# A decoder trunk on one core: the input projection multiplies x scaled by channel weights alone, and one triangular update moves ahead of a scan

## The chip, the cores and the metric

The kernel runs on one core of a Trainium2 chip. Its engines work side by side and meet at semaphores: TensorE (PE) multiplies into eight PSUM banks, VectorE (DVE), ScalarE (ACT) and GpSimd (POOL) work elementwise, SyncE (SP) issues the DMAs. The metric is the device time of one execution, in microseconds.

## What is computed

One decoder layer in float32 on 256 tokens of 1024 channels. This case is about its first part, the mixing block:

```
h = rms_norm(x, norm_pre_mix)        # x * rsqrt(mean(x*x) + 1e-6) * gain
proj = h @ w_in
u_s5, p_ml, p_rw, p_mb = split_cols(proj, (GW, ML_COLS, RW_COLS, MB_COLS))
y = concat(s5_mixer(u_s5), mlstm_mixer(p_ml), rwkv7_mixer(p_rw), moba_mixer(p_mb))
x = x + rms_norm(rms_norm_per_group(y) @ w_out, norm_post_mix)
```

Every mixer begins with work that is linear in its part of `proj`: RWKV mixes each token with the one before it, the mLSTM has a short convolution, S5 a recurrence whose states come from a scan. Attention to 256 memory tokens and a gated feed-forward block follow.

## The kernel before

**Split products.** Each large float32 product is made of three cheaper ones. An operand is split into a rounded `high` (a ScalarE copy) and a `rest` = value - high (a VectorE subtraction), and `mm3` multiplies high by high, high by rest and rest by high. Weights come in slots of 1 MB, loaded by SyncE into a ring of two slots up to `S_WOUT`. A slot is two halves; `high_part` (L344, ScalarE) and `rest` (L350, VectorE) split a half, and `split_channel_major` multiplies it in 24 matmuls of 256 columns. A slot of the ring is loaded again when both of its halves have a rest. Small products (RWKV's solve, S5, the gates) are plain float32.

**The order** is written by hand, engine by engine, and each engine works strictly in it. `highs(n)` and `rests(n)` put the splits of weight halves below n at a place of it. Halves 0 to 17 belong to `rw_wag`, `rw_k`, `rw_r`, `rw_v`, `s5_u`, `ml_q`, `ml_k`, `ml_v`, `ml_o`; from `H_MID` = 18 come `mb_q`, `mb_k`, `mb_v` and the memory's projections.

**The start.** SyncE loads x, two small tables, the first two slots, the rest of the tables. ScalarE and VectorE square x and add its tiles (L362), one TensorE product sums over channels, ScalarE makes the inverse root `rstd_x`, VectorE multiplies x by gain and root in place (L1487), x is split (L1106, L1483), and TensorE begins `rw_wag`.

**Projected groups.** TensorE fills a bank; `shifted` (ScalarE, L1059) copies it times 1 - mu; `mix` (VectorE, L1513) adds the token before; then the bank is free. `conv_now` and `conv_back` do likewise for `ml_q` and `ml_k`.

**RWKV's triangular solve** doubles block sizes over six levels. `level_p` (TensorE) multiplies masked blocks (masks by GpSimd, `level_mask`), `level_x` multiplies them into X and its transpose T, and `level_update` (VectorE, L1656 and L1658) subtracts these from `X` and `XT`. `level_p(2, 0)` needs `level_update(1)`'s first two subtractions: bank 5 holds X of chunk 0 and bank 4 its transpose. `level_x(1, ...)` makes them just before.

**S5.** For each of four pairs: a product, `rotate` (GpSimd), `scan` (VectorE, L1627 and L1628), `rotate_back` (GpSimd, L1006), `s5_out` (TensorE).

## Time and profile before

| what | us |
|---|---|
| median of 3 runs | 527.93 |
| lowest and highest | 526.81, 528.66 |
| the profiled execution | 526.82 |
| its span in the profile | 525.0 |

TensorE is busy for 489.0 us of the span (93%), VectorE for 378.7, ScalarE for 261.2, GpSimd for 172.1. The profile names engines PE, DVE, ACT, POOL and SP; L with a number is a line of the kernel. Matmuls overlap, so their pace is the distance between starts, not a duration.

### The profile page before, as it was taken

Reading aid. Unit: us, or ns where it says so; the run is one execution under the profiler, and the core shown is the slowest. Engines: PE = TensorE matmul, PEld = TensorE weight load, DVE = VectorE, ACT = ScalarE, POOL = GpSimd, SP = SyncE. Lnnn points to the kernel's source line nnn. Section 1 sums busy time; section 2 is a strip of 40 time slices with the busy share of each in tenths; the row PEclk is TensorE's granted clock in tenths of the full one; section 3 lists DMA queues with packets and bytes.
Section 4 is the critical chain, followed back from the end, with each engine's and each line's share of the span. In section 5 each row is a group of like instructions: output and inputs, shape, how many; then the busy total and the mean of one; then the engine's idle time right before and its main releaser. Section 6 shows DMA issues by size and latency. Waiting matters only on the chain.

```text
span 525.0 us, 8449 instructions
## 1 busy us (share of the span) xinstructions
PE 489.0 (93%) x3478; PEld 447.8 (85%) x3478; DVE 378.7 (72%) x443; ACT 261.2 (50%) x410; POOL 172.1 (33%) x103
## 2 busy tenths in 40 slices
PE   0799999889999999999999995999999999999986
PEld 0789989788898888878999884999999999988874
DVE  5675897997766987679655457589999999962114
ACT  3598774331633244657945547454444443443333
POOL 0030317397669250000000001254433443353440
PEclk9999999989999999999999997899999999999999
DMA  8837328022041023535545241356445555545602
GB/s 345 365 96 248 120 93 308 1 81 81 9 153 53 31 81 116 205 99 223 191 171 201 80 150 40 132 199 236 168 161 168 196 198 180 205 161 196 222 0 81
DMA packets 12358, 79.33 MB, mean 151 GB/s; under 512 B 1440, under 2 KB 2080, under 8 KB 3488
## 3 DMA queue, kind: packets, MB, share of 16 engines
q1 hardware_dynamic: 12320, 78.79, 42.3%
q8 instruction: 28, 0.46, 0.4%
q14 instruction: 10, 0.08, 0.1%
HBM read 76.95 MB, written 1.84 MB: 150 GB/s over the span
## 4 chain that ended last, share of the span: by engine, by line
PE 83%; DVE 9%; ACT 3%; issue 2%; DMA 1%; POOLq 0%; POOL 0%; SPq 0%; DVEq 0%; ACTq 0%
PE bank L369 81%; DMA ring<-weights 1%; DVE arena L1635 1%; DVE vx L1662 1%; ACT w_high L344 1%; DVE arena L1452 1%; PE bank L857 1%; POOLq L89 0%; POOL w_rest L350 0%; DVE arena L1627 0%; DVE we_rest L350 0%; DVE arena L1628 0%; DVE wk_rest L350 0%; DVE arena L1806 0%; DVE wm_rest L350 0%
## 5 line engine op out<-in xcount | busy, mean ns | idle before, releaser
L344 ACT ACTIVATE w_high<-ring 128x1024 fp32r<-128x1024 f32 x70 | 73.6, 1058 | 79.7 <-PE bank L369 79.7
L369 PE MATMUL bank<-h_high,w_high 128*128 128x256 f32 x384 | 103.0, 284 | 0.0
L369 PE MATMUL bank<-h_rest,w_high 128*128 128x256 f32 x352 | 99.7, 283 | 0.0
L369 PE MATMUL bank<-h_high,w_rest 128*128 128x256 f32 x320 | 90.7, 283 | 0.0
L350 DVE TENSOR_TENSOR w_rest<-ring,w_high 128x1024 fp32r<-128x1024 f32 x42 | 53.5, 1279 | 44.2 <-ACT w_high L344 44.1
L350 POOL TENSOR_TENSOR w_rest<-third_slot,w_high 128x1024 fp32r<-128x1024 f32 x11 | 26.5, 2407 | 161.4 <-ACT w_high L344 161.4
L350 POOL TENSOR_TENSOR w_rest<-ring,w_high 128x1024 fp32r<-128x1024 f32 x22 | 53.6, 2438 | 74.8 <-ACT w_high L344 74.8
L369 PEld LDWEIGHTS bank<-h_high,w_high 128*128 128x128 f32 x384 | 71.7, 192 | 0.5 <-issue 0.4
L369 PEld LDWEIGHTS bank<-h_rest,w_high 128*128 128x128 f32 x352 | 67.6, 192 | 0.0
L369 PE MATMUL bank<-arena 128*128 128x128 f32 (+7 forms) x496 | 59.4, 300 | 6.5 <-DVE arena L1658 4.5
L369 PEld LDWEIGHTS bank<-arena 128*128 128x128 f32 (+3 forms) x496 | 52.9, 183 | 12.6 <-DVE arena L1658 5.1
L369 PEld LDWEIGHTS bank<-h_high,w_rest 128*128 128x128 f32 x320 | 61.5, 192 | 0.0
L344 ACT ACTIVATE w_high<-third_slot 128x1024 fp32r<-128x1024 f32 x30 | 31.2, 1055 | 28.6 <-PE bank L369 28.6
L369 PE MATMUL bank<-h_high,we_high 128*128 128x256 f32 x128 | 38.3, 299 | 5.7 <-DVE h_rest L1483 5.7
L1452 DVE RECIPROCAL fft<-fft 128x512 f32<-128x512 f32 (+1 forms) x12 | 37.0, 3087 | 0.4
L369 PE MATMUL bank<-h_rest,we_high 128*128 128x256 f32 x128 | 37.3, 291 | 0.0
L369 PE MATMUL bank<-h_high,we_rest 128*128 128x256 f32 x128 | 37.2, 291 | 0.0
L350 DVE TENSOR_TENSOR w_rest<-third_slot,w_high 128x1024 fp32r<-128x1024 f32 x19 | 23.8, 1262 | 17.0 <-ACT w_high L344 17.0
L369 PE MATMUL bank<-w_high,act_high 128*128 128x512 f32 x88 | 34.5, 392 | 1.5 <-POOL w_rest L350 1.5
L369 PE MATMUL bank<-w_rest,act_high 128*128 128x512 f32 x88 | 34.3, 390 | 0.0
L369 PE MATMUL bank<-w_high,act_rest 128*128 128x512 f32 x88 | 34.3, 389 | 0.0
L369 PEld LDWEIGHTS bank<-h_high,we_high 128*128 128x128 f32 x128 | 25.7, 201 | 7.2 <-issue 7.1
(308 smaller groups left out, 1227.2 us busy)
## 6 DMA issues: line engine op xcount, KB each, us to landing
ring<-weights SPq DMA_DIRECT2D x50, 1024.0 KB, 4.9
third_slot<-weights SPq DMA_DIRECT2D x15, 1024.0 KB, 4.9
cst<-consts SPq DMA_DIRECT2D x1, 1664.0 KB, 12.3
gain<-gains SPq DMA_DIRECT2D x3, 512.0 KB, 5.9
par<-params SPq DMA_DIRECT2D x1, 1168.0 KB, 14.6
kx<-x_t SPq DMA_DIRECT2D x1, 1024.0 KB, 4.9
vx<-mem_t SPq DMA_DIRECT2D x1, 1024.0 KB, 10.3
xres<-x_rows SPq DMA_DIRECT2D x1, 1024.0 KB, 10.5
```

The costliest lines, as they stand in the source:

```text
L344: nc.scalar.activation(split_half(i)[0], raw_half(i), ACT.Copy).then_inc(S["w_high"], 1)
L350: e.tensor_tensor(rest_, raw_half(i), high.bitcast(F32), ALU.subtract).then_inc(rest_done(i)[0], 1)
L369: return nc.tensor.matmul(out_, lhsT, rhs, start=start, stop=stop, skip_group_check=True)
L857: last = nc.tensor.transpose(o[:, k, :], xtmp[:, m, c * P:(c + 1) * P], const("ident"))
L1452: return v.reciprocal(x, x)
L1635: v.tensor_tensor(v3(A[:, i, :], 256), v3(o[:, :], 256), copies(mask2, 2), ALU.mult).then_inc(free_of(f"A{i}"), 1)
L1662: last = v.scalar_tensor_tensor(mem_h[:, k, :], mem_h[:, k, :], prm("norm_mem")[:, k:k + 1], rstd_m, ALU.mult, ALU.mult)
```

## The change

**The input norm.** rms_norm of a token is a factor of that token alone, so `proj` = root x ((x x gain) @ w_in). The change splits x x gain directly, in eight tiles of 256 columns (`x_high`, `x_rest`), and gives the root to the projected groups. `x_scale` (VectorE, in place in PSUM) multiplies `rw_wag`, `rw_k`, `rw_r`, `rw_v`, `ml_q`, `ml_k`, `gates` and `ml_o`, and ScalarE's shift, convolution or exponential of the group waits for it. `project_scaled` (VectorE) takes the place of ScalarE's copies of `s5_u` and `mb_k`. The groups whose rows are tokens (`ml_v`, `mb_v`) and the scores of `mb_q` get the root as a column, `rstd_col` and `q_col`, made from two more products of one column. `w_gate` is multiplied by the gain once.

**The start.** The parameters and `onehot` (33 rows) come first, then x and slot 0 in halves, slot 1, the table with `ones`, slot 2, the other constants, slot 3, the other parameters; memory comes with slot 6. TensorE's four `rel` products stand first. The sum over x's squares comes between the halves of `rw_k`, in bank 2. The memory's square moves behind ScalarE's sines, its sum behind `ml_q`.

**Moves in the solve.** `level_update(1)` stands ahead of `rests(H_MID + 4)` and `scan(0)`; GpSimd's `level_mask(3)` ahead of `rotate_back(0)`; `solution(1)` ahead of S5's sigmoid; the product `gn_s5` one step of `w_out` later.

Order of TensorE, start of the program, before (`we0` to `we3` are buffers of w_in halves; numbered banks):

```order
L369 MATMUL bank0<-arena,cst 128x256 [waits x_summed,first_in]
L369 MATMUL bank1<-h_high,we0_high 128x256 [waits h_rest,w_rest_even]
...
L369 MATMUL bank1<-h_high,we1_high 128x256 [waits h_rest,w_rest_odd]
...
L369 MATMUL bank0<-h_high,we2_high 128x256 [waits w_rest_even,bank_free0]
...
L369 MATMUL bank0<-h_high,we3_high 128x256 [waits w_rest_odd]
...
L369 MATMUL bank4<-cst,par 128x384 [waits params_in,consts_in]
```

and in the change:

```order
L378 MATMUL bank4<-cst,par 128x384 [waits onehot_in,first_in]
...
L378 MATMUL bank1<-h_high,we0_high 128x256 [waits h_rest,w_rest_even]
...
L378 MATMUL bank1<-h_high,we1_high 128x256 [waits h_rest,w_rest_odd]
...
L378 MATMUL bank0<-h_high,we2_high 128x256 [waits w_rest_even]
...
L378 MATMUL bank2<-arena,cst 128x256 [waits x_summed,ones_in]
L378 MATMUL bank2<-cst,arena 128x1 x2
L378 MATMUL bank0<-h_high,we3_high 128x256 [waits w_rest_odd]
```

The sum over squares no longer stands ahead of the projection; the `rel` products do.

Order of VectorE between `ml_k` and RWKV's products, before:

```order
L350 TENSOR_TENSOR we0_rest<-ring,we0_high 128x1024 [waits w_high]
L1610 TENSOR_TENSOR arena<-arena 128x512 [waits rw_E,rw_k2]
...
L350 TENSOR_TENSOR wk_rest<-ring,wk_high 128x1024 [waits w_high]
L1618 SCALAR_TENSOR_TENSOR arena<-arena,par 128x256 [waits rw_tilde]
...
L1635 TENSOR_TENSOR arena<-bank4,cst 128x512 [waits bank_full4]
```

and in the change (L1529 is `x_scale`, on `ml_k`, `gates` and `ml_o`):

```order
L1529 TENSOR_TENSOR bank1<-bank1,arena 128x512 [waits bank_full1,rstd_x]
L359 TENSOR_TENSOR we0_rest<-ring,we0_high 128x1024 [waits w_high]
L1582 SCALAR_TENSOR_TENSOR arena<-bank1,par,arena 128x255 [waits bank_full1,ml_cur]
...
L1529 TENSOR_TENSOR bank2<-bank2,arena 36x256 [waits bank_full2,rstd_x]
...
L1687 SCALAR_TENSOR_TENSOR arena<-arena,par 128x256 [waits rw_tilde]
...
L1529 TENSOR_TENSOR bank1<-bank1,arena 128x512 [waits bank_full1,rstd_x]
L1705 TENSOR_TENSOR arena<-bank4,cst 128x512 [waits bank_full4]
```

Three scalings have come in, and the first stands between `ml_k` and the weight half that follows it.

Order of VectorE at the first level update (L1627 and L1628 are the scan's), before:

```order
L1662 SCALAR_TENSOR_TENSOR vx<-vx,par,arena 128x256 [waits rstd_m]
...
L1627 SCALAR_TENSOR_TENSOR arena<-small,arena 128x256 [waits rotating]
L1628 SCALAR_TENSOR_TENSOR arena<-small,arena 128x256
...
L350 TENSOR_TENSOR wm_rest<-ring,wm_high 128x1024 [waits w_high]
L350 TENSOR_TENSOR wk_rest<-ring,wk_high 128x1024 [waits w_high]
L1656 TENSOR_TENSOR arena<-arena,bank5 128x512 [waits bank_full5]
```

and in the change:

```order
L1732 SCALAR_TENSOR_TENSOR vx<-vx,par,arena 128x256 [waits rstd_m]
...
L359 TENSOR_TENSOR wm_rest<-ring,wm_high 128x1024 [waits w_high]
L1726 TENSOR_TENSOR arena<-arena,bank5 128x512 [waits bank_full5]
L1728 TENSOR_TENSOR arena<-arena,bank4 128x512 [waits bank_full4]
...
L359 TENSOR_TENSOR wk_rest<-ring,wk_high 128x1024 [waits w_high]
L1697 SCALAR_TENSOR_TENSOR arena<-small,arena 128x256 [waits rotating]
```

Four scans and a weight split now stand behind the update.

The diff, cut to its core:

```diff
+            def x_high(k):
+                a.activation(h_split[0][:, k, :], hT[:, k, :], ACT.Copy,
+                             scale=prm("pre_mix")[:, k:k + 1]).then_inc(S["h_high"], 1)
+            for k in range(4):
+                x_high(k)
+            highs(1)
+            act.wait_ge(S["x_high_in"], 16)
+            for k in range(4, KD):
+                x_high(k)
+            highs(2)
+            x_square(0)
+            highs(4)
+            x_square(1)
+            a.activation(step, prm("log_step"), ACT.Exp).then_inc(S["s5_step"], 1)
+            highs(5)
...
+            def x_scale(name, rows_=P, n=2):
+                dve.wait_ge(S["rstd_x"], 1)
+                o = v3(wait_full(dve, name)[0:rows_, 0:n * T], T)
+                v.tensor_tensor(o, o, copies(rstd_x[0:rows_], n), ALU.mult).then_inc(S["x_scaled"], 1)
+            def project_scaled(name, out_):
+                o = v3(wait_full(dve, name)[:, :], T)
+                v.tensor_tensor(out_, o, copies(rstd_x, 2), ALU.mult).then_inc(free_of(name), 1)
...
+            x_scale("ml_q")
             rests(14)
...
             rests(16)
+            x_scale("ml_k")
+            rests(17)
             conv_back(1, "ml_k")
-            rests(17)
+            x_scale("gates", GATES, 1)
...
+            rests(H_MID + 3)
+            level_update(1)
+            rests(H_MID + 4)
             scan(0)
-            rests(H_MID + 4)
-            level_update(1)
...
             rests(H_WKV + 10)
+            solution(1)
+            rests(H_WKV + 11)
             dve.wait_ge(S["s5_exp"], 1)
```

## Rows read from the trace of the kernel before

**Rows 1.** TensorE's waits, whole span: waiter <- releaser: us in total, times, longest

```profile
PE bank L369 <- DVE arena L362: 9.6, 1, 9.6
PE bank L369 <- DVE h_rest L1483: 5.7, 1, 5.7
PE bank L369 <- DVE arena L1658: 4.5, 2, 4.0
...
PE bank L857 <- DVE xtmp L1880: 2.4, 1, 2.4
...
PE bank L369 <- DVE arena L1752: 1.3, 1, 1.3
...
PE bank L369 <- ACT arena L1229: 0.8, 1, 0.8
```

**Rows 2.** the chain that ended last, whole span: start us, us, what

```profile
8.89 1.06 ACT we_high L344
...
16.42 35.73 PE bank L369 x257
```

**Rows 3.** DMA issues, 0 to 60 us: count, KB each, us to landing

```profile
kx<-x_t SPq DMA_DIRECT2D x1, 1024.0 KB, 4.9
...
par<-params SPq DMA_DIRECT2D x1, 56.0 KB, 4.4
```

**Rows 4.** timeline (start us, us, engine, line), `rw_wag`'s matmuls at each rate

```profile
17.20 0.42 PE L369 MATMUL bank<-h_high,we_high 128*128 128x256 f32 x1
...
17.41 0.41 PE L369 MATMUL bank<-h_rest,we_high 128*128 128x256 f32 x1
...
22.00 0.28 PE L369 MATMUL bank<-h_high,we_high 128*128 128x256 f32 x1
...
22.11 0.28 PE L369 MATMUL bank<-h_rest,we_high 128*128 128x256 f32 x1
```

**Rows 5.** TensorE's timeline of 30 to 33.5 us, the `rel` products

```profile
30.36 2.84 PE L369 MATMUL bank<-cst,par 33*128 33x384 f32 x8
```

**Rows 6.** ScalarE's timeline, 20 to 60 us; in brackets the idle before, its releaser

```profile
24.91 0.82 ACT L1059 ACTIVATE arena<-bank,small 128x256 f32<-128x256 f32 x2
25.62 2.00 ACT L344 ACTIVATE we_high<-ring 128x1024 fp32r<-128x1024 f32 x2
...
52.17 1.57 ACT L1146 ACTIVATE arena<-bank,small 128x256 f32<-128x256 f32 x4 [2.18 <-PE bank L369]
```

**Rows 7.** VectorE's timeline, around 57 us

```profile
57.44 2.36 DVE L350 TENSOR_TENSOR we_rest<-ring,we_high 128x1024 fp32r<-128x1024 f32 x2 [0.83 <-ACT we_high L344]
```

**Rows 8.** VectorE's timeline, 60 to 100 us

```profile
84.39 4.87 DVE L1635 TENSOR_TENSOR arena<-bank,cst 128x512 f32<-128x512 f32 x8 [2.53 <-PE bank L369]
```

**Rows 9.** VectorE's timeline, 100 to 107 us

```profile
99.96 0.68 DVE L1627 TENSOR_TENSOR_SCAN arena<-small,arena 128x256 f32<-128x256 f32 x1
...
102.31 1.19 DVE L350 TENSOR_TENSOR wm_rest<-ring,wm_high 128x1024 fp32r<-128x1024 f32 x1
103.42 2.28 DVE L350 TENSOR_TENSOR wk_rest<-ring,wk_high 128x1024 fp32r<-128x1024 f32 x1
...
106.22 0.67 DVE L1658 TENSOR_TENSOR arena<-arena,bank 128x512 f32<-128x512 f32 x1
```

**Rows 10.** TensorE's timeline, fp32 level products ahead of the wait and behind it

```profile
99.14 3.84 PE L369 MATMUL bank<-arena 128*128 128x128 f32 x32
...
106.95 3.64 PE L369 MATMUL bank<-arena 128*128 128x128 f32 x16 [3.97 <-DVE arena L1658]
```

**Rows 11.** stretches: PE, PEld, DVE, ACT, POOL busy, granted clock, DMA share, GB/s

```profile
107.00:108.00 1.00, 1.00 (x5) 1.00 (x6) 1.00 (x2) 0.00 (x0) 1.00 (x1) 0.50 0.35 123
204.00:206.00 2.00, 0.73 (x12) 0.66 (x13) 2.00 (x5) 1.54 (x2) 0.00 (x0) 1.00 0.00 0
322.00:323.00 1.00, 0.81 (x4) 0.85 (x5) 1.00 (x3) 1.00 (x2) 0.00 (x0) 0.50 0.00 0
```

**Rows 12.** GpSimd's timeline, 60 to 210 us: turning S5's first pair back

```profile
102.46 7.10 POOL L1006 TENSOR_TENSOR arena<-arena 128x512 f32<-128x512 f32 x4 [2.71 <-DVE arena L1628]
```

More of the change, by code:

```diff
@@ L302, in wait_slot, with scaled @@
             return slot(n)
+        SCALED = ["rw_wag", "rw_k", "rw_r", "rw_v", "ml_q", "ml_k", "gates", "ml_o"]
+        def scaled(eng, name):
+            eng.wait_ge(S["x_scaled"], SCALED.index(name) + 1)
+            return bank[uses[name][0]]
         half_user = {}
@@ L575, in _ @@
                 mm(o[:, 0:384], prm("rel", 33)[:, h:h + 1].to_broadcast([33, P]), const("onehot", 33)).then_inc(full[4 + h], 1)
-            split_channel_major(2, "rw_r", 1, h_split)
-            o = pe_open(pe, "mem_sumsq", 7)
-            pe.wait_ge(S["mem_summed"], 3)
-            mm(o[:, 0:T], const("ones"), sq_m[:, 0, :]).then_inc(full[7], 1)
+            split_channel_major(0, "rw_wag", 1, h_split, lambda j: pe.wait_ge(S["h_rest"], j + 1))
+            split_channel_major(1, "rw_k", 0, h_split, None, (0,))
+            o = pe_open(pe, "x_sumsq", 2)
+            pe.wait_ge(S["ones_in"], 16)
+            pe.wait_ge(S["x_summed"], 3)
+            mm(o[:, 0:T], const("ones"), sq_x[:, 0, :])
+            for m in range(2):
+                last = mm(o[:, T + m:T + m + 1], sq_x[:, 0, m * P:(m + 1) * P], const("ones")[:, 0:1])
+            last.then_inc(full[2], 1)
+            split_channel_major(1, "rw_k", 0, h_split, None, (1,))
+            split_channel_major(2, "rw_r", 3, h_split)
             split_channel_major(3, "rw_v", 0, h_split)
@@ L597, in _ @@
             split_channel_major(5, "ml_q", 0, h_split)
+            o = pe_open(pe, "mem_sumsq", 7)
+            pe.wait_ge(S["mem_summed"], 3)
+            mm(o[:, 0:T], const("ones"), sq_m[:, 0, :]).then_inc(full[7], 1)
             o = pe_open(pe, "rw_kk", 3)
@@ L1165, in _ @@
             a.activation(rwE[:, 2], Gp, ACT.Exp, scale=-1.0).then_inc(S["rw_E"], 1)
-            o = wait_full(act, "gates")
+            o = scaled(act, "gates")
             a.activation(rows[0][0:NH, :], o[32:32 + NH, 0:T], ACT.Identity,
@@ L1186, in _ @@
             a.activation(E_[:, 0:1024], flat(cv), ACT.Tanh, scale=0.5).then_inc(S["ml_silu"], 1)
-            o = wait_full(act, "ml_o")
+            o = scaled(act, "ml_o")
             a.activation(mlo, v3(o[:, :], T), ACT.Exp, scale=-1.0).then_inc(free_of("ml_o"), 1)
@@ L1201, in _ @@
             highs(H_MID + 5)
-            project("mb_k", mqk[:, 2:4, :])
             highs(H_MID + 6)
@@ L1529, in conv_back @@
                     last.then_inc(S["ml_conv"] if d < 3 else free_of(name), 1)
+            rests(5)
+            x_scale("rw_wag")
             mix(0, "rw_wag")
             rests(6)
+            x_scale("rw_k")
             mix(1, "rw_k")
@@ L1541, in _ @@
             v.tensor_scalar(rwE[:, 0, 1, :], rwE[:, 0, 1, :], 0.5, 0.5, ALU.mult, ALU.add).then_inc(S["rw_lowrank"], 1)
+            x_scale("rw_v")
+            rests(11)
             mix(3, "rw_v")
             rests(12)
+            dve.wait_ge(S["consts_in"], 16)
+            dve.wait_ge(S["params_in"], 16)
+            w_gate = v3(prm("w_gate"), GATES)
+            v.tensor_tensor(w_gate, w_gate, spread(prm("pre_mix"), GATES), ALU.mult).then_inc(S["gate_gain"], 1)
             moved(dve, "rw_k")
@@ L1620, in _ @@
             last.then_inc(S["rw_bonus"], 1)
+            x_scale("ml_o")
             def scan(q):
@@ L1691, in _ @@
             rests(H_MID + 6)
+            project_scaled("mb_k", mqk[:, 2:4, :])
             scan(1)
@@ L1817, in _ @@
             v.tensor_tensor(z5, z5y, z5b, ALU.mult).then_inc(S["s5_z"], 1)
-            rests(H_WKV + 11)
-            solution(1)
             group_gain(1, "ml")
```

147 lines of the change are left out of this document (81 added, 66 removed).

## The prediction

> **What bounds the kernel now.** I began with TensorE's waits [rows 1]. TensorE is the busiest engine, and the time that it lacks sits in few places: 9.6 and 5.7 us at the start, 4.0 us (the longest of two) at the level update, and short waits after. Then I read the chain [rows 2]: nothing but TensorE stands in it from 16.42 us on for 35.73 us, so the start is bound by what makes the first operands, and the next 35 us by TensorE's own pace. The last view is the timeline of the engines that feed it. ScalarE works almost without a pause from 24.91 to 50.0 us (52.17 less its 2.18 of idle, [rows 6]), and VectorE from 57.44 us to 81.86 (84.39 less 2.53, [rows 7, 8]). So both feeders have little room, and that decides what an earlier start is worth.
>
> **The start.** The parameters (56 KB, 4.4 us to landing though behind x, [rows 3]) now go first, so the `rel` products begin at 4.0 to 5.1 us. At the higher rate they took 2.8 us [rows 5]. The first matmuls here come 0.21 us apart, later ones 0.11 to 0.12 [rows 4]: 256 columns at 1.2 GHz, then near 2.4. So `rel` takes some 5.6 us and ends at about 10. Half of x, issued 0.9 us later than all of it before (landed 0.72 + 4.9, [rows 3]), is there by 5.5. Four `x_high` at 0.41 us (half of 0.82, [rows 6]), one weight half at about 1.0 (half of 2.00, [rows 6]) and its rest at 1.2 (half of 2.36, [rows 7]) end at 9.2. `rw_wag` begins at 10 instead of 16.42, probably at the full clock, since `rel` has worked for 5.6 us by then, about as long as it took before. Added to `rel` out of the way later (2.8) and 2.2 us of slow matmuls, the lead of TensorE's stream would be 11 us, if the feeders kept up.
>
> They don't. The root now comes late: ScalarE does eight tiles, four halves and two squares first (14.3 us), VectorE its three sums by 17.4, TensorE reaches the product at 18.6, and the root is there at 20.5. `x_scale` on a 512-column bank is costed at 0.61 us, from VectorE's nearest row that reads PSUM (4.87 for 8, [rows 8]); writing PSUM is in no row, so 0.4 to 1.0. ScalarE's shift of `rw_wag` then starts at 21.2, against 24.91 before [rows 6]: 3.7 us of lead. One weight half is already split: +1.0. At `rw_v` ScalarE waits for VectorE, which has `rests(9)`, a mix and `rests(10)` ahead of that scaling: -1.1. The memory's square is moved in here: -1.9. The tanh of `rw_w` so comes at 50.0 - 3.6 + 1.9 = 48.3 us (52.17 before), and `ml_q` starts 4.0 us earlier than before, not 11.
>
> TensorE gets gaps in between: about 3 us ahead of `rw_v`, 2 ahead of `s5_u`, 3 ahead of `rw_g`. The trace shows what gaps do to the clock: after idles of 3.97 us [rows 10] and 2.4 us [rows 1] the granted clock is 0.50, the 1.2 GHz level; after 1.3 us it stayed 1.00 [rows 1, 11]. The gap ahead of `rw_g` is nearest to these longer ones, and `ml_q` behind it is waited for. The loss there is taken as 1.5 us, what the level products show below. The Trainium skill says so too ("TensorE: Matmul & The Clock Gate", HAM oscillation): an array left idle is throttled to half rate and has to be worked warm again. By that rule the gaps cost time, and the trace agrees at 3.97 us.
>
> So `ml_q` is full at 55.7 + 1.5 = 57.2, its scaling ends at 57.8, and `rests(14)` behind it starts 0.4 us later than its 57.44 [rows 7]. From there VectorE has its 24.4 us of work as before, plus the scalings of `ml_k`, `gates` and `ml_o` (0.6, 0.25, 0.6), plus 1.7 us: ScalarE can shift `ml_k` only behind the scaling, and the weight half that `rests(17)` needs comes after that shift. It reaches the first RWKV bank at 85.4 us against 84.39 [rows 8]: **+1.0**. The whole lead of the start is gone there. What hid such a delay before, 2.53 us of idle [rows 8], is used up.
>
> **The level update.** Before, VectorE ran the scans (99.96 to 102.31: 2.35 us), two rests (1.1 and 2.2) and only then the four subtractions, the second of which (106.22 + 0.67) released TensorE at 106.95 [rows 9, 10]. Now the scans and the second rest stand behind. The second subtraction ends at 106.9 + 1.0 - 2.35 - 2.2 = 103.3. TensorE itself gets there at 99.14 + 3.84 = 102.98 [rows 10], plus 1.0. So it goes on at 104.0, bound by its own stream: **-2.9**. And its clock: 32 level products took 3.84 us ahead of the wait, 16 took 3.64 behind it [rows 10], at a clock of 0.50 [rows 11]. Without the gap 16 take 1.9; with the short wait for chunk 1 counted, **-1.5**. `mb_k` thus starts 4.4 us earlier. The rest that it needs in its second half is done 1 us after the update, well ahead of it.
>
> **Later.** `solution(1)` no longer waits behind S5's sigmoid with its long reciprocal: the 1.3 us wait [rows 1] goes, **-1.3**, and S5's output, 2 to 3 us later on VectorE, is needed 7 us on. `gn_s5` one step later hides most of 0.8 us [rows 1]: **-0.6**. The two extra columns, `w_gate` and the split copies of `ml_v` and `mb_v` are tenths beside other work: 0. The other waits stay, the late ones (2.4, [rows 1]) too.
>
> Sum: -2.9 - 1.5 - 1.3 - 0.6 = -6.3 us. The profiled execution took 526.82; 520.5. The median of the three runs is 1.1 us above it: **521.6**.
>
> **The rivals.**
> *A, the start survives.* If the clock doesn't fall at `ml_q` (1.5) and VectorE's 1.7 us wait is half as long, RWKV's products start 2.3 us earlier: 519.3. For it: `s5_u` may itself run slowly and fill the gap. Against: both feeders are full. At best, with cheap scalings, 517.
> *B, S5 becomes late.* `scan(0)` now ends 4 to 5 us later in its place, GpSimd's turning back takes up to 7.1 us [rows 12], the next rotation, `scan(1)` and the rows behind it on VectorE hang on that, and TensorE waits for the bank at S5's third product, where I count 0 to 3 us. 524.0.
> *C, the hand-overs decide.* Each scaled group goes TensorE, VectorE, ScalarE, VectorE, and each of these is a queue with weight splits in it. Six groups pass before RWKV's products. I count 1.1 + 1.7 us of such waits; if each of the six costs 1.4 us more than I count, VectorE arrives 8.4 us later and 6.3 are more than lost. 530.0, slower. For it: VectorE's queue is full after 57 us. Against: for the first four groups ScalarE is the full engine [rows 6] and VectorE waits for it.
> *D, the swap does nothing.* If X and T of chunk 0 came from TensorE only at 103 us, the update would wait for them wherever it stands; then only the late terms remain and S5's delay eats them: 526.8. Against: TensorE had ended all of `level_x(1)` at 102.98 [rows 10], chunk 0's half of it some 2 us before.
>
> **How the numbers follow.** Forecast 0.46; A 0.22; B 0.18; D 0.07; C 0.07. The range runs from A's best, 517.0, to B with a dearer scaling (0.4 us more in four places), 525.6, and leaves out C, D and a little of A. A measurement here tells about 0.3% (1.6 us) from no change: faster 0.86 (forecast, A, B), the same 0.07 (D), slower 0.07 (C).
>
> **What would show it.** TensorE's first matmul at 4 to 5 us and `rw_wag` at about 10. ScalarE's first shift at about 21, the tanh of `rw_w` near 48. Pauses of 2 to 3 us in TensorE between 27 and 49 us with the granted clock at 0.50 behind one. VectorE's first RWKV bank at 85, within 2 us. No wait above 1 us ahead of the level-2 products and a granted clock of 1.00 there; no wait of TensorE for `solution(1)`. I am wrong if `x_scale` takes over 1 us, if TensorE waits anew for VectorE or GpSimd between 105 and 140 us, or if the lead at the RWKV products is not near zero.

## The result: 529.2 us, 0.4% slower, and the profile after

The changed kernel takes **529.24 us** (median of 20 executions, 527.77 to 534.48) against 527.41 us of the kernel before (median of 20, one of them at 697.66). The ratio is 1.0042, with a 95% interval of 1.0025 to 1.0058: slower by 1.3 to 3.1 us. Forecast was a faster kernel, 521.6 us, and the result lies outside the range. The profiled execution took 528.38 us, its span is 526.6 us at a mean granted clock of 0.983 (before: 526.82, 525.0, 0.985). In the text A is VectorE's first RWKV bank, the row of line 1705 (before: 1635).

TensorE's waits of the changed kernel, to be laid beside [rows 1] (waiter <- releaser: us in total, times, longest):

```profile
PE bank L378 <- DVE we_rest L359: 7.1, 5, 3.3
PE bank L378 <- DVE h_rest L2024: 3.5, 1, 3.5
PE bank L378 <- DMA cst<-consts: 3.0, 1, 3.0
PE bank L378 <- DVE arena L1728: 2.8, 2, 1.9
PE bank L378 <- ACT arena L1195: 2.7, 1, 2.7
PE bank L873 <- DVE xtmp L1953: 2.4, 1, 2.4
...
PE bank L378 <- issue: 1.1, 2, 0.9
PE bank L378 <- POOL arena L1029: 1.0, 1, 1.0
```

The 15.3 us of the start have become 3.0 of DMA, 1.45 ahead of `rw_wag`, 3.3 ahead of `rw_v` and 2.7 ahead of `rw_g`. The 4.0 us at the level update are gone, and so are the two late waits (1.3 and 0.8). But the update's releaser still stands there with 2.8 us (1.9 at level 2, 0.9 at 187 us), and GpSimd's line 1029 and "issue" are new. Summed over the whole table TensorE waits 4 us less than before (26.7 against 30.7) and the kernel is longer: this table alone would say the opposite of the result. Its work has become longer by more than that: `rel` takes 5.46 us at the start, 2.84 before [rows 5], and the clock lost 1.7 us more (the table of the experiments).

Now the start. The first three rows are TensorE's, the fourth to sixth ScalarE's (start us, us, engine, line; in brackets the idle before and its releaser):

```profile
3.03 5.46 PE L378 MATMUL bank<-cst,par 33*128 33x384 f32 x8 [3.03 <-DMA cst<-consts]
9.94 0.58 PE L378 MATMUL bank<-h_high,we_high 128*128 128x256 f32 x1 [1.45 <-DVE we_rest L359]
51.14 2.08 PE L378 MATMUL bank<-arena,par 128*128 128x256 f32 x4 [2.67 <-ACT arena L1195]
...
23.11 0.84 ACT L1082 ACTIVATE arena<-bank,small 128x256 f32<-128x256 f32 x2 [0.40 <-DVE bank L1529]
44.03 0.84 ACT L1082 ACTIVATE arena<-bank,small 128x256 f32<-128x256 f32 x2 [1.18 <-DVE bank L1529]
50.26 1.56 ACT L1195 ACTIVATE arena<-bank,small 128x256 f32<-128x256 f32 x4
```

And stretches of the same trace (PE, PEld, DVE, ACT, POOL busy with counts, granted clock, DMA share, GB/s):

```profile
12.00:14.00 2.00, 2.00 (x14) 2.00 (x13) 1.20 (x1) 1.86 (x2) 0.00 (x0) 1.00 0.11 37
14.00:16.00 2.00, 2.00 (x19) 2.00 (x19) 1.87 (x2) 2.00 (x4) 0.00 (x0) 1.00 0.82 266
34.00:36.00 2.00, 2.00 (x11) 2.00 (x10) 2.00 (x2) 1.97 (x4) 0.00 (x0) 0.50 0.41 49
52.00:54.00 2.00, 2.00 (x8) 1.73 (x8) 1.97 (x2) 1.99 (x2) 1.92 (x2) 0.50 0.57 242
```

`rw_wag` begins at 9.94, 6.5 us earlier than the 16.42 of [rows 2]. ScalarE's first shift is 1.8 us earlier than in [rows 6], its tanh 1.9 us. VectorE then has nothing left of it:

```profile
59.62 0.70 DVE L1529 TENSOR_TENSOR bank<-bank,arena 128x512 f32<-128x512 f32 x1 [1.92 <-PE bank L378]
60.23 2.35 DVE L359 TENSOR_TENSOR we_rest<-ring,we_high 128x1024 fp32r<-128x1024 f32 x2
...
75.55 1.23 DVE L359 TENSOR_TENSOR we_rest<-ring,we_high 128x1024 fp32r<-128x1024 f32 x1 [1.85 <-ACT we_high L353]
...
87.25 0.68 DVE L1529 TENSOR_TENSOR bank<-bank,arena 128x512 f32<-128x512 f32 x1
87.86 4.86 DVE L1705 TENSOR_TENSOR arena<-bank,cst 128x512 f32<-128x512 f32 x8
```

The rests that began at 57.44 [rows 7] begin at 60.23, A at 87.86 instead of 84.39 [rows 8]: 3.5 us late, without the 2.53 us of idle that stood there.

From there to 145 us, TensorE first, then VectorE, then GpSimd:

```profile
102.61 6.22 PE L378 MATMUL bank<-arena 128*128 128x128 f32 x48
108.58 0.36 PE L378 MATMUL bank<-h_high,wm_high 128*128 128x256 f32 x1
...
119.11 0.62 PE L378 MATMUL bank<-arena,par 128*32 128x256 f32 x4 [0.96 <-POOL arena L1029]
...
122.96 2.35 PE L378 MATMUL bank<-arena 128*128 128x128 f32 x16 [1.93 <-DVE arena L1728]
...
139.89 1.13 PE L378 MATMUL bank<-arena 128*128 128x128 f32 x8 [0.20 <-issue]
141.92 1.13 PE L378 MATMUL bank<-arena 128*128 128x128 f32 x8 [0.90 <-issue]
...
105.74 0.67 DVE L1728 TENSOR_TENSOR arena<-arena,bank 128x512 f32<-128x512 f32 x1
...
108.67 1.58 DVE L1697 TENSOR_TENSOR_SCAN arena<-small,arena 128x256 f32<-128x256 f32 x1
110.18 1.51 DVE L1698 TENSOR_TENSOR_SCAN arena<-small,arena 128x256 f32<-128x256 f32 x1
...
107.71 3.43 POOL L1040 TENSOR_TENSOR arena<-arena,cst 128x512 f32<-128x512 f32 x2 [4.30 <-PE bank L378]
112.94 6.03 POOL L1029 TENSOR_TENSOR arena<-arena 128x512 f32<-128x512 f32 x4 [1.79 <-DVE arena L1698]
...
137.72 4.10 POOL L1040 TENSOR_TENSOR arena<-arena,cst 128x512 f32<-128x512 f32 x2
```

The level products that were cut in two by 3.97 us [rows 10] run through: all 48 in 6.22 us. `mb_k` starts at 108.58 against 110.35 (110.35 is its start in the trace of before), 1.8 us early although A is 3.5 us late: the swap won 5.3 us. Behind it stand two waits that before had none, 0.96 on GpSimd's turning back and 1.93 on the second update. Two shorter ones follow (0.20 and 0.90), for which the profile names no releaser. The program has TensorE wait there for GpSimd's `level_mask(4)`, and TensorE goes on 0.1 us behind each of its two masks (line 1040, ends at 139.78 and 141.82; before they had ended at 133.60). They stand behind the second turning back, which is late too, and each took 2.1 us instead of 1.1, beside VectorE's split of `vx` (3.30 us instead of 2.35). The first `H_WKV` group starts at 144.83 instead of 141.87, 3.0 us late. So 4.8 us are given back between 109 and 145 us. The rest of the kernel wins 1.4 us, and 1.6 us late is the end.

### The profile page after: what moved, and what is told of

It reads as the page before. It is cut to its first block, busy times and chain, and to the rows that moved or that the text cites. A ratio compares the mean times of both kernels' runs of the same rounds, so it can differ in the third digit from the quotient of the medians.

```text
span 526.6 us, 8491 instructions
## 1 busy us (share of the span) xinstructions
PE 494.4 (94%) x3482; PEld 450.1 (85%) x3482; DVE 384.6 (73%) x451; ACT 263.2 (50%) x420; POOL 172.5 (33%) x103
## 4 chain that ended last, share of the span: by engine, by line
PE 74%; DVE 14%; ACT 5%; issue 5%; DMA 1%; POOLq 0%; POOL 0%; DVEq 0%; SPq 0%; ACTq 0%
PE bank L378 73%; DVE we_rest L359 2%; ACT we_high L353 1%; DVE vx L1732 1%; DVE arena L1705 1%; DVE arena L1582 1%; DMA kx<-x_t 1%; DVE bank L1529 1%; DVE wm_rest L359 1%; DVE arena L1697 1%; ACT arena L1167 1%; DVE arena L1698 1%; PE bank L873 1%; ACT arena L1082 1%; DVE arena L1728 0%
## 5 line engine op out<-in xcount | busy, mean ns | idle before, releaser
L378 PEld LDWEIGHTS bank<-h_rest,w_high 128*128 128x128 f32 x352 | 67.6, 192 | 0.0
L378 PEld LDWEIGHTS bank<-arena 128*128 128x128 f32 (+3 forms) x496 | 51.6, 178 | 11.7 <-DVE arena L1728 4.4
## 6 DMA issues: line engine op xcount, KB each, us to landing
par<-params SPq DMA_DIRECT2D x1, 1168.0 KB, 11.5
```

Of the source, the lines that this page charges most:

```text
L378: return nc.tensor.matmul(out_, lhsT, rhs, start=start, stop=stop, skip_group_check=True)
```

## The experiments

Sixteen kernels, in four groups (e1 to e4, e5 to e8, e9 to e12, e13 to e16) that each ran on one chip beside the kernel before. The changed kernel was in none of them, and the median of the kernel before was 527.27 to 527.77 us in the groups, so differences between groups are uncertain by about 0.5 us more. Executions of one kernel spread over up to 6.7 us, and the slower ones have the lower mean clock. So the last column gives, for the profiled execution, its time and how much clock it lost: one less the granted clock, summed over the span without the last fall, which every trace has just before its end (6.8 us of it in the kernel before, at 526.82).

| kernel | median us (executions) | ratio to before | interval | profiled: us, clock lost |
|---|---|---|---|---|
| changed kernel | 529.24 (20) | 1.0042 | 1.0025 to 1.0058 | 528.38, 8.5 |
| e1 swap alone | 527.06 (12) | 0.9999 | 0.9982 to 1.0016 | 527.35, 6.8 |
| e2 two late moves alone | 524.42 (5) | 0.9945 | 0.9929 to 0.9960 | 523.93, 5.1 |
| e3 both | 526.55 (11) | 0.9978 | 0.9963 to 0.9993 | 526.89, 10.2 |
| e4 norm alone | 533.01 (4) | 1.0111 | 1.0092 to 1.0130 | 532.77, 11.9 |
| e5 changed, no scalings | 522.07 (4) | 0.9895 | 0.9876 to 0.9914 | 524.10, 8.5 |
| e16 the same again | 523.27 (6) | 0.9908 | 0.9887 to 0.9930 | 525.25, 11.9 |
| e12 changed, scalings aside | 526.76 (10) | 0.9990 | 0.9972 to 1.0008 | 524.69, 8.5 |
| e15 the same again | 526.41 (12) | 0.9990 | 0.9967 to 1.0012 | 528.44, 13.6 |
| e13 changed, late four scalings only | 525.83 (12) | 0.9963 | 0.9951 to 0.9975 | 526.67, 6.8 |
| e14 changed, early four only | 525.58 (12) | 0.9978 | 0.9955 to 1.0001 | 525.65, 11.9 |
| e6 changed, pauses filled | 531.84 (4) | 1.0086 | 1.0072 to 1.0100 | 531.92, 10.2 |
| e11 changed, filled ahead of `rw_wag` | 528.36 (10) | 1.0022 | 0.9998 to 1.0045 | 527.34, 8.5 |
| e7 e3 with two more moves | 525.62 (5) | 0.9963 | 0.9950 to 0.9975 | 525.62, 8.5 |
| e8 e2 and half the swap | 522.26 (4) | 0.9903 | 0.9889 to 0.9916 | 522.29, 3.4 |
| e9 e8 with update(2) earlier | 522.32 (6) | 0.9906 | 0.9891 to 0.9921 | 520.97, 3.4 |
| e10 changed, half the swap | 529.04 (12) | 1.0017 | 1.0002 to 1.0033 | 526.03, 8.5 |

### The parts apart: e1 to e4

**e1** is the kernel before with the swap alone, on VectorE and on GpSimd:

```diff
+            rests(H_MID + 3)
+            level_update(1)
+            rests(H_MID + 4)
             scan(0)
-            rests(H_MID + 4)
-            level_update(1)
...
+            level_mask(3)
             rotate_back(0)
-            level_mask(3)
```

> The kernel before with the swap alone: level_update(1) ahead of rests(H_MID+4) and scan(0) on VectorE, level_mask(3) ahead of rotate_back(0) on GpSimd. Theory (the swap pays at the level update and gives part back behind it, because scan(0), the rows behind it and GpSimd's turning back come late): mb_k starts about 4.5 us earlier than before (110.35), mb_v only 1 to 2 us earlier than 125.72, the first memory product about 0 to 1 us earlier, and the time is 0 to 1 us below before. Rival (the swap pays in full, and the loss comes from the input norm alone): the whole 4.5 us stay to the end, ratio 0.991.

Measured: 0.9999, no difference. Its trace (TensorE, then a stretch):

```profile
105.17 0.36 PE L369 MATMUL bank<-h_high,wm_high 128*128 128x256 f32 x1
...
115.68 0.62 PE L369 MATMUL bank<-arena,par 128*32 128x256 f32 x4 [0.94 <-POOL arena L1006]
...
119.53 2.35 PE L369 MATMUL bank<-arena 128*128 128x128 f32 x16 [1.93 <-DVE arena L1658]
...
124.00:128.00 4.00, 4.00 (x23) 4.00 (x24) 1.22 (x3) 0.00 (x0) 2.67 (x3) 0.60 0.48 203
```

`mb_k` is 5.2 us early, though A is at 84.86 here, 0.5 us late; the prediction's two terms, without the 1.0 us that A was to be late, are 5.4. The same two waits as in the changed kernel follow, and behind them the clock falls to a mean of 0.60, so that `mb_v`'s first half takes 4.64 us instead of 3.14. At the first `H_WKV` group (142.06, before 141.87) all is gone. This happens without any of the norm's work: the swap gives back what it wins.

**e2** is the kernel before with `solution(1)` ahead of S5's sigmoid and `gn_s5` one step later:

```diff
             rests(H_WKV + 10)
+            solution(1)
+            rests(H_WKV + 11)
             dve.wait_ge(S["s5_exp"], 1)
...
-                if kt == 0:
+                if kt == 1:
                     group_sumsq("gn_s5", 0, 3)
```

> The kernel before with the two late moves alone: solution(1) ahead of S5's sigmoid, gn_s5 one step of w_out later. Theory: TensorE's waits of 1.3 and 0.8 us go, 1.3 to 1.9 us faster, ratio 0.997. Rival: what follows (S5's output, RWKV's tail) comes later by as much and TensorE waits there instead, ratio 1.000.

Measured: 0.9945, 2.9 us, more than the 1.9 of the prediction. Both waits (1.3 and 0.8) are gone from the table of waits; the one for line 1951 has grown from 3.3 to 4.0. The rest is clock: the profiled execution lost 1.7 us less of it, all behind 320 us (granted clock 0.72 over 320 to 332 us, 0.58 before).

**e3** is e1 and e2 together.

> The kernel before with the swap and the late moves, without the input norm. Theory: the sum of the two parts, 1.5 to 3 us faster, ratio 0.995 to 0.997. Rival (the swap pays in full): 6 us faster, ratio 0.988.

Measured: 0.9978. With the swap on top, e2 is 2.1 us worse. In its profiled execution the clock falls already at 120 us (0.53 over 120 to 130), and the first `H_WKV` group is 2.3 us late.

**e4** is the changed kernel with all moves undone: the norm alone, that is parameters first, split of the raw x, scaled groups.

```diff
-            rests(H_MID + 3)
+            scan(0)
+            rests(H_MID + 4)
             level_update(1)
-            rests(H_MID + 4)
-            scan(0)
...
-            solution(1)
-            rests(H_WKV + 11)
             dve.wait_ge(S["s5_exp"], 1)
...
+            rests(H_WKV + 11)
+            solution(1)
```

> The changed kernel with the swap and the late moves undone: the input norm's change alone. Theory (the lead of the start is lost to ScalarE and VectorE, which get the scalings and the hand-overs): VectorE reaches the first RWKV bank at 87 to 88 us instead of 84.39, and the whole shift of 3 to 4 us stays, since the level update is bound by VectorE: 3 to 4 us slower than before, ratio 1.006 to 1.008. Rival (the norm is neutral, the moves cost): ratio 1.000.

Measured: 1.0111, 5.8 us **slower**. A is at 88.41, and the wait that the swap was to remove is longer than before:

```profile
88.41 4.26 DVE L1705 TENSOR_TENSOR arena<-bank,cst 128x512 f32<-128x512 f32 x7
...
111.56 3.78 PE L378 MATMUL bank<-arena 128*128 128x128 f32 x16 [4.56 <-DVE arena L1728]
```

`mb_k` starts at 114.99 (4.6 us late) and nothing regains it. So the norm is the harmful part. VectorE is 4.0 us late at A, and that lateness reaches the update whole, because VectorE's own chain (masks, subtractions, memory, scans, update) runs without a gap from A to the update. At the end it is 6.0 us in the profile, with 5.1 us more of lost clock.

### The norm: e5, e12, e13 to e16, e6, e11

**e5** leaves out the eight scalings, so these groups lack the root. **e12** leaves VectorE their time, on other data, and takes away only the hand-over (the groups stay unscaled here too):

```diff
 e5:
-                dve.wait_ge(S["rstd_x"], 1)
-                o = v3(wait_full(dve, name)[0:rows_, 0:n * T], T)
-                v.tensor_tensor(o, o, copies(rstd_x[0:rows_], n), ALU.mult).then_inc(S["x_scaled"], 1)
+                return
 e12:
...
-                v.tensor_tensor(o, o, copies(rstd_x[0:rows_], n), ALU.mult).then_inc(S["x_scaled"], 1)
+                v.tensor_tensor(v3(scratch[0:rows_, 0:n * T], T), copies(rstd_x[0:rows_], n), copies(rstd_x[0:rows_], n),
+                                ALU.mult).then_inc(S["x_scaled"], 1)
 both, on ScalarE:
-                o = v3(scaled(act, name)[:, :], T)
+                o = v3(wait_full(act, name)[:, :], T)
```

> The changed kernel without the eight scalings of x_scale: the readers take the banks straight from TensorE, so seven projections of x and the output gate stay without 1/rms (the output is another one; times only). Takes away 8 operations of 0.6 to 0.7 us (the gates' one shorter) on VectorE and the waits of ScalarE behind them (1.18 us at rw_v, up to 8.6 us of idle ahead of ml_k's shift, which is mostly slack). Feeder theory (VectorE's and ScalarE's queues carry the late arrival at RWKV's first bank): that bank comes 3 to 5 us earlier than the changed kernel's 87.86, and the whole is 524 to 526 us. Clock theory (the low clock of rw_wag and the gaps ahead of rw_v and rw_g carry it): the bank comes at most 1.5 us earlier, 527.5 to 529 us.

> The changed kernel with the eight scalings at their places in VectorE's queue and of the same shape, but on other data into a buffer that nobody reads, and with ScalarE taking the banks straight from TensorE: VectorE has the scalings' time, the hand-over TensorE, VectorE, ScalarE is gone (the groups stay unscaled, so the output is another one). It splits the 7.2 us between the changed kernel and the one without scalings (522.1). If VectorE's time for them is the price (8 of 0.6 to 0.7 us, the gates' one 0.4, 4.9 us in all): 526.5 to 528 us, the RWKV bank at 86.5 to 87.5. If ScalarE's wait behind the scaling is: 522.5 to 524.5 us, the bank at 84 to 85.

Measured: 522.07 and 526.76 against 529.24. A, in e5 and then in e12:

```profile
83.30 1.89 DVE L1702 TENSOR_TENSOR arena<-bank,cst 128x512 f32<-128x512 f32 x3 [2.03 <-PE bank L377]
```

```profile
83.66 1.87 DVE L1710 TENSOR_TENSOR arena<-bank,cst 128x512 f32<-128x512 f32 x3
```

By e5 the scalings cost 7.2 us. How that divides, the two numbers of e12 answer differently: its median (4.7 us above e5) says VectorE's time, its A (0.36 us behind e5's, 4.2 ahead of the changed kernel's) says hand-over, each with what was expected of it. **e15** and **e16** are e12 and e5 once more, side by side:

> e12_aside once more, beside e16_no_scale on one chip (both leave the eight groups unscaled). If e12's slower executions (526.5 to 528.8, mean clock 0.973 to 0.978) were the clock's falls at short pauses behind 115 us and not VectorE's time: its executions at a mean clock of 0.982 and more lie within 1 us of e16's at the same clock, and the medians differ by as much as their clocks do. If VectorE's time is the price: 3.5 to 5 us more than e16 at the same clock too.

> e5_no_scale once more, for the comparison with e15_aside: 521.5 to 524.5 us.

Measured: 526.41 and 523.27, so VectorE's time has a price by the medians again, 3.1 us. It stands at a near mean clock too: 526.26 (six at 0.983) against 522.82 (four at 0.986), and at the same one, 0.982, it is 2.5 us, with one execution of each. But the profiled executions show what it consists of. A is at 82.72 in e15 and 82.42 in e16. e12 and e5, which lost the same 8.5 us of clock, took 524.69 and 524.10. e15 took 3.2 us more than e16 and had lost 1.7 us more clock. So VectorE's time itself costs 0.6 to 1.5 us by these two pairs, since it fills idle of VectorE (2.03 us ahead of A in e5), and the rest of 3 to 5 us goes with clock that falls in more executions and at more places. Between the changed kernel and e12, both with 8.5 us of clock lost, lie 3.7 us: the **hand-over** (2.5 by the medians). These are single profiled executions, so the division is good to a microsecond or so. Of the expectations for e15 neither held whole.

One caution belongs to all comparisons at A. The slow products of the start (see below) last longer in some executions: the first 72 took 10.2 to 11.5 us in the ten traces with the changed start (e11 apart). Counted from the end of these 72, A comes after 67.5 to 67.6 us in the changed kernel, e4 and e10, after 62.4 in e12 and 62.3 in e15, after 61.8 in e5 and 60.7 in e16. So at A the hand-over is 5.2 us, VectorE's time 0.6 to 1.6.

**e13** keeps the scalings of `ml_q`, `ml_k`, the gates and `ml_o` alone, **e14** those of `rw_wag`, `rw_k`, `rw_r` and `rw_v` alone (the others stay unscaled):

```diff
 e13:
-        SCALED = ["rw_wag", "rw_k", "rw_r", "rw_v", "ml_q", "ml_k", "gates", "ml_o"]
+        SCALED = ["ml_q", "ml_k", "gates", "ml_o"]
 e14:
-        SCALED = ["rw_wag", "rw_k", "rw_r", "rw_v", "ml_q", "ml_k", "gates", "ml_o"]
+        SCALED = ["rw_wag", "rw_k", "rw_r", "rw_v"]
 both, in scaled and in x_scale:
+            if name not in SCALED:
+                return wait_full(eng, name)
...
+                if name not in SCALED:
+                    return
```

> The changed kernel without the scalings of rw_wag, rw_k, rw_r and rw_v (these four stay unscaled, so the output is another one); those of ml_q, ml_k, gates and ml_o stay. If the hand-over in ScalarE's full stretch is the price (its wait of 1.18 us at rw_v, the pause of 2.67 us ahead of rw_g with the clock's fall behind it): the tanh of rw_w 1.5 us earlier than 50.26, RWKV's first bank at 85.0 to 86.2 against 87.86, 525 to 526.5 us. If the price is VectorE's time and the hand-over of ml_k behind 57 us: the bank at 87.0 or later, 528 to 529 us.

> The changed kernel with the scalings of rw_wag, rw_k, rw_r and rw_v alone; ml_q, ml_k, the gates and ml_o stay unscaled (another output). It gives back three operations of 0.60, one of 0.33 us and VectorE's wait of 1.85 us for the weight half behind ml_k's shift, 4.0 us in all. If the late stretch carries the price: RWKV's first bank at 84.0 to 85.0 against 87.86, 524 to 525.5 us. If the early one does: the bank at 86 to 87, 527 to 528.5 us.

Measured: 525.83 and 525.58. A, in e13 and then in e14:

```profile
86.40 4.26 DVE L1709 TENSOR_TENSOR arena<-bank,cst 128x512 f32<-128x512 f32 x7
```

```profile
84.52 4.88 DVE L1709 TENSOR_TENSOR arena<-bank,cst 128x512 f32<-128x512 f32 x8 [2.35 <-PE bank L380]
```

Leaving out either half wins 3.4 to 3.7 us by the medians, so both stretches pay, each in its way. The late four cost 3.3 us at A (84.52 against 87.86), and it would be more if VectorE didn't then wait 2.35 us for TensorE: VectorE is full there. The early four cost 1.5 at A: with them ScalarE waits at `rw_v`, the pause ahead of `rw_g` is 2.67 us instead of 0.91, and the clock falls behind it (in e13 it falls once in this stretch, at `s5_u`). Counted from the end of the first 72 products, the late four cost 3.5 us at A and the early four 2.3.

e5 and e16 say one more thing. Without any scaling, on raw x with parameters first, A is 1.1 to 2.0 us earlier than in the kernel before (83.30 and 82.42 against 84.39, [rows 8]), from a stream that starts 6.2 us earlier. Against e3, which has the same moves and no norm, e5 is 4.5 us faster by the medians, e16 3.3. So, under this order of moves, by e5 (by e16 in brackets): all of the norm but the scalings, above all the early start, -4.5 (-3.3), scalings +7.2 (+6.0), together +2.7, and e3's -0.9 (526.55 against 527.4) makes the +1.8 us of the result.

**e6** fills the pauses ahead of `rw_v` (24 products) and `rw_g` (20), **e11** the pause ahead of `rw_wag` (8), with work that nobody reads:

```diff
 e6:
+            moved(pe, "x_sumsq")
+            fill(2, 24)
             split_channel_major(3, "rw_v", 0, h_split)
...
+            moved(pe, "rel2")
+            fill(6, 20)
             o = v3(pe_open(pe, "rw_g", 2)[:, :], T)
 e11, behind the rel products:
+            pe.wait_ge(S["h_high"], 1)
+            for _ in range(8):
+                mm(bank[2][:, 0:T], h_split[0][:, 0, 0:P], h_split[0][:, 0, :])
```

> The changed kernel with 24 needless 256-column products into a bank that nobody reads in TensorE's pause ahead of rw_v, and 20 ahead of rw_g, so that the pauses are filled with work (same result). Clock theory: the clock in 34 to 36 and 51 to 54 us goes from 0.50 to 0.73 up to 1.00, rw_v takes 5.5 to 6 us instead of 7.47 and rw_g under 1.5, ml_q is full 1.5 to 2.5 us earlier, RWKV's first bank comes 1.5 us earlier, 527 to 528 us. Feeder theory: the groups that follow start when the weight halves are split, ml_q moves by under 1 us, RWKV's first bank by under 0.7 us, 528.5 to 529.5 us. If the products run at the low rate and hold up rw_v, slower than 530.

> The changed kernel with eight needless 256-column products between rel and rw_wag, in the 1.45 us in which TensorE stands idle (same result). If that pause is why the first third of rw_wag runs at half pace in the changed kernel (72 products in 10.40 us, 8.9 at the full pace): rw_wag ends 1.0 to 1.5 us earlier, the root and ScalarE's first shift as much, and VectorE's first RWKV bank 0.8 to 1.5 us earlier than 87.86; 527.7 to 528.4 us. If the slow pace has nothing to do with the pause: rw_wag takes 10.4 to 11.5 us again, 529 to 530 us.

Measured: e6 531.84, 2.6 us **slower** than the changed kernel. `rw_v` did run at the full rate (48 products in 5.98 instead of 7.47 us) and `rw_g` too (1.03 instead of 2.08), but then `s5_u` met a pause of 2.23 us and took 7.49 instead of 5.99, and `ml_q`'s scaling began at 60.53 instead of 59.62. Warming one group moved the pause and the low rate to the next one, as in e5 and e13, where `rw_v` ran at the full rate and `s5_u` then took 7.46 and 7.48 us. But the fillers aren't shown to be what made e6 slower. Its start had the longest run of slow products: the first shift came at 24.36, 1.25 us behind the changed kernel's and ahead of any filler, and A only 0.92 behind (88.78). Most of the rest arises later, where the granted clock was 0.72 over 120 to 138 us and 1.00 in the changed kernel, behind the same two waits. Counted from the end of the first 72 products, A is 0.3 us earlier than in the changed kernel, where 1.5 was expected: as a cure, filling does nearly nothing here.

e11 is 528.36, 0.9 us faster than the changed kernel by the medians, though the intervals overlap. The first 72 products (`rw_wag` and half of `rw_k`) took 9.55 us instead of 10.40, but could start only at 10.51, since the fillers (8.45 to 10.52) outlasted the pause: the shift came 0.28 us earlier, not 1.0 to 1.5. Its profile shows something else. The pause ahead of `rw_g` is the same to 0.01 us, yet the clock stayed up:

```profile
50.88 1.13 PE L378 MATMUL bank<-arena,par 128*128 128x256 f32 x4 [2.68 <-ACT arena L1198]
```

```profile
51.00:54.00 3.00, 3.00 (x23) 2.90 (x24) 2.97 (x2) 2.97 (x5) 2.92 (x2) 1.00 0.69 276
```

From the start of `rw_g` to the end of `ml_q`'s products it takes 6.88 us (50.88 to 57.76), 8.37 in the changed kernel (51.14 to 59.51). The fall of the clock is thus 1.5 us, and A comes 1.7 us earlier (86.12): 1.5 of it is the clock. That is the price the prediction gave the fall, met to a tenth.

### The order at the level update: e7 to e10

**e7** is e3 with `level_update(2)` ahead of the rest of half `H_MID+5` and of the conv product, and `level_mask(4)` ahead of `rotate_back(1)`:

```diff
+            level_update(2)
+            rests(H_MID + 5)
             dve.wait_ge(S["ml_silu"], 1)
...
-
-            rests(H_MID + 5)
-            level_update(2)
             rests(H_MID + 6)
...
+            level_mask(4)
             rotate_back(1)
-            level_mask(4)
```

> The kernel before with all of the change's moves behind 100 us and without its norm, and, where the moves alone made TensorE wait anew, two more: level_update(2) ahead of the rest of half H_MID+5 and of the conv product on VectorE, and level_mask(4) ahead of the turning back of chunk 1 on GpSimd. If the new waits are all that ate the swap's 5 us: the 1.9 us wait ahead of mb_v goes and with it the clock's fall behind it, the level-3 waits shrink, 520 to 522 us. If S5's chain (scan(0) late, turning back, scan(1), s5_out) sets the end of this stretch however the updates are ordered: the wait for the turned-back chunk stays or grows by what is gained, 524 to 526 us.

**e8** is e2 with half the swap: the update ahead of the long rest, but behind the scans, and GpSimd as before:

```diff
             scan(0)
+            level_update(1)
             rests(H_MID + 4)
-            level_update(1)
```

> The kernel before with solution(1) and gn_s5 moved as in the change, and level_update(1) moved ahead of the rest of half H_MID+4 only: scan(0) and GpSimd's order stay as they were, so S5 is as early as before. The update comes 2.2 us earlier. If S5's lateness is what ate the swap: no new wait ahead of s5_out, mb_k 2.5 to 3.5 us earlier than 110.35 (with the shorter gap the clock may stay up), and 1.5 to 2.5 us of it are kept: 522 to 523 us against 524.4 with the two late moves alone. If whatever is won at level 1 is lost again at level 2 (VectorE's rests and the level-2 update come when they come): 524 to 525 us.

Measured: e7 525.62, e8 **522.26**. In e7 the wait for the second update is gone (0.5 in all is left on that line), and 2.48 us on line 1702 has come in its place: the rows behind `scan(1)`, which hang on GpSimd's rotation, which hangs on the late `scan(0)`. S5's chain is the limit there once the update isn't. In e8 it isn't late:

```profile
100.15 0.68 DVE L1627 TENSOR_TENSOR_SCAN arena<-small,arena 128x256 f32<-128x256 f32 x1
...
103.80 2.35 PE L369 MATMUL bank<-arena 128*128 128x128 f32 x16 [0.62 <-DVE arena L1658]
106.38 0.36 PE L369 MATMUL bank<-h_high,wm_high 128*128 128x256 f32 x1 [0.22 <-DVE wm_rest L350]
...
119.31 2.35 PE L369 MATMUL bank<-arena 128*128 128x128 f32 x16 [1.52 <-DVE arena L1658]
```

The wait of 3.97 us is 0.62, the 16 products behind it take 2.35 us instead of 3.64 [rows 10], `mb_k` is 4.0 us early. No wait for S5's bank follows, one of 1.52 us for the second update does, and 2.1 us are still there at the first `H_WKV` group (139.79 against 141.87). Half the swap keeps 2.2 us over e2; the whole swap loses 2.1 (e3). The half that was added, `scan(0)` behind the update and GpSimd's mask ahead of `rotate_back(0)`, is what turns it. No run has these two apart, but in the changed kernel's rows GpSimd had ended its mask and stood idle for 1.79 us until the scan was done, so it is the scan that holds up the turning back; the mask beside it made the scan 1.8 us longer (4.1 instead of 2.35).

**e9** is e8 with the second update ahead of one rest; **e10** is the changed kernel with e8's order:

```diff
 e9:
+            level_update(2)
             rests(H_MID + 5)
-            level_update(2)
 e10:
+            scan(0)
             level_update(1)
             rests(H_MID + 4)
-            scan(0)
...
+            rotate_back(0)
             level_mask(3)
-            rotate_back(0)
```

> e8_half_swap with level_update(2) ahead of the rest of half H_MID+5 on VectorE (1.21 us) as well. In e8 TensorE waits 1.52 us ahead of the level-2 products for that update, and the rest is needed only at mb_v, 4 us later. If each order that leaves scan(0) and GpSimd alone is kept: that wait falls to about 0.4 us and the whole to 521.2 to 521.5 us against e8's 522.3. If S5's chain is by now the limit of this stretch: a wait at the level-3 products or at S5's rotated chunk takes its place, 522.0 to 522.5 us.

> The changed kernel with the half swap instead of its swap: on VectorE scan(0), then level_update(1), then the rest of half H_MID+4; on GpSimd rotate_back(0) ahead of level_mask(3), as before. If the swap's order was its own loss and the norm's price is the same under any order: the norm alone (533.0) plus what e8 gained (-5.1), 527.5 to 528.3 us, against 529.2 of the changed kernel. If the later arrival of VectorE makes TensorE wait for the update again, with the clock's fall behind it: 529.5 to 531 us.

Measured: e9 522.32, the same as e8. Its wait is down to 0.37 us as expected and its profiled execution is the fastest of all (520.97), but half of its executions show a mean clock of 0.985 to 0.988 and take 522.5 to 523.3. e10 is 529.04, between the two expectations: 527.5 to 528.3 was for a price that doesn't depend on the order, 529.5 to 531 for a new wait with the clock's fall. Its A is as late as in the changed kernel (87.68), so TensorE waits again:

```profile
108.62 3.66 PE L378 MATMUL bank<-arena 128*128 128x128 f32 x16 [2.35 <-DVE arena L1728]
```

and the clock falls behind it. Its executions lie at 526.0 to 527.3 (four, clock 0.981 to 0.983) or at 528.4 to 529.7 (eight, 0.976 to 0.979). The norm and the order interact: with VectorE late, each of the two orders gives either a late update or a late S5. The version that beats both kernels is e8, without the norm, 1.0% faster than before.

## Why the prediction was wrong, by its own steps

The profiled execution was to take 520.5 us and took 528.4. Two steps of the prediction failed: the start at the full clock, and "the other waits stay" behind the level update. The 7.9 us are three terms: 2.6 at `mb_k` (108.58, forecast 110.35 - 4.4 = 105.95), 4.8 between `mb_k` and the first `H_WKV` group, 0.5 in the rest.

- **What bounds the kernel** was read rightly: both feeders are full, and an earlier start is worth little at A, 1.1 to 2.0 us by e5 and e16, with no scaling at all.
- **The start** was right up to the clock. `rel` took 5.5 us, as forecast, though from 3.0 on instead of 4.0 to 5.1, and `rw_wag` began at 9.94 (forecast 10). "Probably at the full clock" is the step that failed: the first 72 products (`rw_wag` and half of `rw_k`) took 10.40 us, at half pace until 13.3 us (8.88 for the next 72, so 1.5 us lost), in e5, e6, e12 and e16 even 11.3 to 11.5. The root's products ran at 20.2 to 21.1, not at 18.6, and the shift came at 23.11, not 21.2: **1.9 us**. From there the working holds to some tenths: the tanh 2.0 late on it (50.26, forecast 48.3), `ml_q`'s scaling 59.6 (forecast 57.2), A 87.86 (forecast 85.4). The error at A is 2.5 us, of which the start made 1.9.
- **The scalings** were costed at 0.61 us and are 0.60 to 0.70. The waits at `rw_v` (1.1, measured 1.18) and at the weight half behind `ml_k`'s shift (1.7, measured 1.85) are there. The pauses of 3 us ahead of `rw_v` and `rw_g` are 3.3 and 2.7; the 2 us ahead of `s5_u` are 0.7. The clock loss at `ml_q` (1.5) is 1.5. So the terms hold one by one; their balance against the start's lead doesn't, since that lead was 1.9 us smaller. In place of +1.0 at A stands +3.5, and e4 shows where that goes under the old order: 4.0 us late at A, 6.0 at the end of the profile.
- **The level update** was right: no gap, a granted clock of 1.00, 4.4 us forecast for `mb_k` with A 1.0 late, 1.8 measured with A 3.5 late. In e1, with A 0.5 late, it is 5.2.
- **Later** is the second step that failed, and the larger: I wrote "the other waits stay" behind the update and gave S5's lateness to rival B, at 0 to 3 us of TensorE's wait. The measured waits are 0.96 and 1.93, within that, but the price is 4.8: 1.1 more are the two stops for `level_mask(4)`, the last 0.8 is spread over the products around them. B named the chain: `scan(0)` later, turning back, the next rotation, `scan(1)` and the rows. The turning back was not dearer (6.03 against 7.10 us, [rows 12]). What B left out is the scan itself, which took 4.1 us instead of 2.35 beside `level_mask(3)` on GpSimd, that the second update stands behind the rows, which stand behind that scan, and that the second turning back makes the next masks late; and in e1 and e3 the clock's fall.
- **The late moves** were 1.9 us in the sum, 2.9 by e2, whose waits fell by 1.4 net; the rest is clock that the sum did not have.
- **Rival C**, the only one on the slower side, had the hand-overs 8.4 us dearer than counted. They cost 3.7 us in all, 2.8 of which the sum had: that its total (530.0) came near is luck. **Rival D** falls in e1: the update did not wait for TensorE. **Rival A** falls with the start.

In all: B's chain at 4.8 us, and 2.6 at `mb_k`, 1.9 of which came with the late first shift. For the profiled execution B alone would have given 525.3, the start alone 523.1, both still faster than before; I had given the cases chances as if one excluded the other, and the range stopped at the first.

## What to carry to other kernels

When work is brought forward to end a wait of the busiest engine, price what it now stands ahead *of*, down to the next two waits of that engine: here the half of the swap that passed a weight rest kept 2.2 us, and the half that passed the scan lost it and 2.1 more. A change that removes a wait at the start and adds small operations to a feeder pays for them, once the feeder's idle is used up (here 2.53 us ahead of A), at the next place where that feeder is waited for; the table of waits gets shorter while the kernel gets longer. And of a change with several parts, run each alone: two late moves of a few lines were worth 2.9 us, hidden under a large part that cost 5.8.
